# Neighbourhood attention of the second block in steps of two heads, with row-half score matmuls on split operands and one add-and-minimum instruction

## The reference

```python
s_loc = einsum(q, k_band) * scale + bias          # bias from rpb by relative row and column
s_loc = where(in_win, s_loc, -inf)                 # 16 columns around the query
s_ctx = einsum(q, k_ctx) * scale
p = softmax(concatenate([s_loc, s_ctx], -1))
o = einsum(p_loc, v_band) + einsum(p_ctx, v_ctx)
```

## Time and profile before

| | us |
|---|---|
| median of 3 runs | 3548.5 (3540.64 to 3551.41) |
| the profiled execution | 3541.35, its span 3539.6 |
| PE, PEld, DVE, ACT, POOL busy | 3237.2, 2082.1, 1327.0, 1012.4, 233.2 |

### The profile page before, as it was taken

One profiled execution on the slowest core, in us unless ns is written; L12 is line 12 of the kernel. 1 busy time (PEld: TensorE's weight loads), 2 busy tenths in 40 slices (PEclk: granted clock), 3 DMA queues, 4 the chain that ended last, 5 costly groups with the idle time before them and its releaser, 6 DMA issues.

```text
span 3539.6 us, 38820 instructions
## 1 busy us (share of the span) xinstructions
PE 3237.2 (91%) x15536; PEld 2082.1 (59%) x15536; DVE 1327.0 (37%) x2224; ACT 1012.4 (29%) x1976; POOL 233.2 (7%) x224
## 2 busy tenths in 40 slices
PE   7999979998999979988999878999999998869998
PEld 3555644534555545433666446888788565448886
DVE  2452231223552322121433754333323333563444
ACT  2452211111551211123123444222222222343332
POOL 0010000000000100000022001000001022000000
PEclk9999989998999989998999999999999999989999
DMA  4011238871002248885210001333232210013221
GB/s 165 25 37 49 72 120 356 357 323 50 35 25 78 77 200 336 366 343 211 71 36 25 13 1 72 119 119 119 109 118 76 99 41 26 1 61 105 97 95 48
DMA packets 62001, 413.62 MB, mean 117 GB/s; under 512 B 7504, under 2 KB 8016, under 8 KB 14464
## 3 DMA queue, kind: packets, MB, share of 16 engines
q1 hardware_dynamic: 55664, 392.06, 28.7%
q0 software_dynamic: 5008, 16.98, 1.4%
q10 hardware_dynamic: 1152, 2.10, 0.2%
HBM read 409.01 MB, written 2.10 MB: 116 GB/s over the span
## 4 chain that ended last, share of the span: by engine, by line
PE 85%; DVE 8%; ACT 3%; issue 2%; POOL 1%; DMA 1%; DVEq 0%; ACTq 0%; SPq 0%; POOLq 0%
PE bank L644 82%; PE bank L645 3%; DVE arena L1798 3%; ACT arena L1292 3%; DVE x L1798 1%; DMA weight<-in_ada_w 0%; POOL arena L2471 0%; POOL arena L2481 0%; POOL arena L2413 0%; DVE arena L2031 0%; DVE arena L2333 0%; DVE arena L2029 0%; DVE tokens_low L1798 0%; DMA weight<-in_w_up 0%; DVE arena L2049 0%
## 5 line engine op out<-in xcount | busy, mean ns | idle before, releaser
L644 PE MATMUL bank<-arena,weight 128*128 128x512 f32 (+2 forms) x2080 | 826.4, 555 | 59.1 <-DVE arena L1798 42.0
L1292 ACT ACTIVATE arena<-bank 128x512 f32<-128x512 f32 (+5 forms) x746 | 374.5, 520 | 1690.2 <-PE bank L644 1394.7
L644 PE MATMUL bank<-arena 128*64 128x128 f32 (+4 forms) x3888 | 620.6, 342 | 54.7 <-ACT arena L1292 23.7
L644 PEld LDWEIGHTS bank<-arena,weight 128*128 128x128 f32 (+1 forms) x2080 | 392.7, 191 | 469.9 <-issue 427.5
L644 PE MATMUL bank<-weight,arena 128*64 128x512 f32 (+5 forms) x2936 | 608.8, 530 | 33.0 <-ACT arena L1292 9.7
L644 PEld LDWEIGHTS bank<-arena 128*128 128x128 f32 (+2 forms) x3888 | 399.7, 170 | 238.5 <-issue 142.8
L644 PEld LDWEIGHTS bank<-weight,arena 128*64 128x64 f32 (+2 forms) x2936 | 294.9, 150 | 316.2 <-issue 261.3
L644 PE MATMUL bank<-hidden,weight_part 128*128 128x512 f32 (+1 forms) x2304 | 446.4, 355 | 0.0
L644 PE MATMUL bank<-tokens_high,weight_part 128*128 128x512 f32 (+1 forms) x1536 | 420.6, 359 | 23.9 <-DVE tokens_low L1798 23.7
L644 PEld LDWEIGHTS bank<-hidden,weight_part 128*128 128x128 f32 x2304 | 381.1, 189 | 70.3 <-DVE arena L1798 3.5
L644 PEld LDWEIGHTS bank<-tokens_high,weight_part 128*128 128x128 f32 x1536 | 276.5, 191 | 82.7 <-DVE tokens_low L1798 30.4
(11 more groups left out here) (115 smaller groups left out, 1676.7 us busy)
## 6 DMA issues: line engine op xcount, KB each, us to landing
weight<-in_w_gate SPq DMA_DIRECT2D x64, 1024.0 KB, 13.8
weight<-in_w_up SPq DMA_DIRECT2D x64, 1024.0 KB, 6.7
weight<-in_w_down SPq DMA_DIRECT2D x64, 1024.0 KB, 10.1
weight<-in_w_ff SPq DMA_DIRECT2D x64, 1024.0 KB, 5.0
weight<-in_ada_w SPq DMA_DIRECT2D x48, 1024.0 KB, 5.5
weight<-in_w_in SPq DMA_DIRECT2D x26, 1024.0 KB, 6.1
weight<-in_w_o SPq DMA_DIRECT2D x8, 1024.0 KB, 4.8
weight<-in_w_mem_kv SPq DMA_DIRECT2D x8, 1024.0 KB, 4.8
```

The lines of the kernel that those rows point to most:

```text
L644: mm = lambda o, a, b, first=True, last=True: eng.matmul(o, a, b, start=first, stop=last, skip_group_check=True)
L1292: act = lambda o, i, f=ACT.Copy, **k: eng.activation(o, i, f, **k)
```

## The change

In the neighbourhood attention of both layers of the second block:

- The queries are scaled by -1/8 and, like the keys, stored as a high and a low fp32r part (ACT writes the high part, DVE the low one). `Q` and the zero-padded `KZ` are gone, and POOL's clearing of `KZ` with them.
- A step is a pair of heads. The scores are three matmuls for each head on its own 64 rows, the heads taking turns, 512 columns for both heads and then 256 for both.
- The scores and the bias have the other sign: mask +1e30, `MASK - b` on POOL, and the minimum in place of the maximum. One `tensor_tensor_reduce` adds the bias and takes the minimum of 512; a second one does the 256 context scores against a zero, starting from the first one's minimum. ACT's copy, DVE's reduction over 768 and its negation are gone.
- The exponential is `exp(-x + min)` and not divided; `attend_blocks` is used, with the division at the end through `shares` and `out_scaled`. Half of the transposed tiles are copied down by DVE.
- `MASK`, the zero, the `BM` slots and `RB` lie in buffers that all stages of the block have (`AC`, `SQ`, `N`). There are still two `BM` slots, and POOL's loop is as it was but for the operation.

```diff
+                def na_score(pu):
+                    kind, _, j, q = pu
+                    at = q * P + (0 if kind == "n" else T)
+                    for name, keys in (("S", slice(0, T)), ("Sc", slice(T, T + CT))):
+                        if name == "S" and kind == "nc":
+                            continue
+                        o = [take_bank((name, u)) for u in heads_of(pu)]
+                        for n, (a, b) in enumerate((("QH", "KH"), ("QH", "KL"), ("QL", "KH"))):
+                            for h in range(2):
+                                r = slice(64 * h, 64 * h + 64)
+                                i = mm(o[h][:, 0:keys.stop - keys.start], S[a][r, j, at:at + P], S[b][r, j, keys], n == 0, n == 2)
...
+                attend_blocks(na_blocks(l), S, na_score, ..., beside(2))
...
+                def na_exps(pu):
...
+                    for u in heads_of(pu):
+                        eng.wait_ge(*after(("nb", u)))
+                        p, at = S["PR"].get(u), 2 * pu[3] + u[4]
+                        src = p if pu[0] == "n" else PB.get(("Sc", u))[:, 0:CT]
+                        act(p if pu[0] == "n" else p[:, 0:CT], src, ACT.Exp, bias=S["ST"].get(u)[:, 0:1], scale=-1.0,
+                            accum_out=r[:, at:at + 1])...
...
+                def na_tops(pu):
+                    for u in heads_of(pu):
...
+                        eng.wait_ge(*after(("out", ("S", u))))
+                        eng.wait_ge(*after(("bm", u)))
+                        eng.tensor_tensor_reduce(p[:, 0:T], PB.get(("S", u)), S["BM"].get(u), 1.0, 3.0e38, ADD, ALU.min,
+                                                 s[:, 0:1]).then_inc(*done(PB.free(("S", u)), S["BM"].free(u)))
+                        eng.wait_ge(vector_step, done.count)
+                        eng.wait_ge(*after(("out", ("Sc", u))))
+                        eng.tensor_tensor_reduce(p[:, T:T + CT], PB.get(("Sc", u))[:, 0:CT], S["ZERO"].broadcast_to([P, CT]), 1.0, s[:, 0:1], ADD, ALU.min,
+                                                 s[:, 0:1]).then_inc(*done(PB.free(("Sc", u)), ("nb", u)))
...
-                eng.memset(S["KZ"], 0.0).then_inc(*done(("nz", l)))
...
-                    eng.tensor_tensor(b, b, S["MASK"], ADD).then_inc(*done(("bm", us[n])))
+                    eng.tensor_tensor(b, S["MASK"], b, SUB).then_inc(*done(("bm", us[n])))
```

More of the change, by code:

```diff
@@ L144, in constants @@
     inside = (kc >= start) & (kc < start + 16)
-    mask = np.where(inside, 0.0, -1e30).astype(f)
+    mask = np.where(inside, 0.0, 1e30).astype(f)
     mask = np.tile(mask, (2, ROWS))
@@ L544, in build @@
             t = f".na{l}"
-            b = dict(H=H, YG=Y2, Q=c(2, T + CT), KZ=c(4, T + CT), V=c(6, 256), MASK=c(T), BM=c.ring("BM" + t, 2, T), **com)
-            b.update(attention(c, t, T + CT, 4, 5))
+            b = dict(H=H, YG=Y2, **{n: c.rounded(f"na_{n}{l}", 2, T + CT) for n in ("QH", "QL", "KH", "KL")}, V=c(6, 256),
+                     MASK=com["AC"].slots[0], ZERO=com["AC"].slots[1][:, 0:1], BM=Ring(st, "BM" + t, com["SQ"].slots), **com)
+            b.update(paired(c, t, T + CT, 4, (2, 2), [com["N"]]))
             B["na", l] = b
@@ L579, in build, with na_blocks @@
         PREP_AT = [NG - 4, NG - 2] + [NG + 4 * j + 2 * h for j in range(3) for h in range(2)]
-        def na_units(l):
-            return units("n", l, range(2), TB) + (units("nc", l, range(2), 2) if l == 0 else [])
+        def na_blocks(l):
+            return blocks_of("n", l, range(2), TB) + (blocks_of("nc", l, range(2), 2) if l == 0 else [])
         def df_units(l, j):
@@ L1184, in _ @@
                 project_rows("nv", "w_nv", 6)
-                for key in [("nqc", l, j, i) for j in range(2) for i in range(1 + both)]:
+                for key in [("nql", l, j, i) for j in range(2) for i in range(1 + both)]:
                     eng.wait_ge(*after(key))
-                for key in [("nkc", l, h, i) for h in range(4) for i in range(2)]:
+                for key in [("nkl", l, j, i) for j in range(2) for i in range(2)]:
                     eng.wait_ge(*after(key))
@@ L1356, in shares, with attend_blocks @@
                     eng.wait_ge(*after(S["RB"].former))
-                copy(b, ("rb", okey), PB.get(("rb", okey)), ("rbc", okey))
-            def attend_blocks(pus, S, n, okey, nq, between=None, turn_lag=1, value_lag=2):
+                copy(b[:, 0:nq * P], ("rb", okey), PB.get(("rb", okey))[:, 0:nq * P], ("rbc", okey))
+            def attend_blocks(pus, S, one, blocks, okey, nq, between=None, turn_lag=1, value_lag=2):
                 for i in range(len(pus) + value_lag):
@@ L1631, in _, with high @@
                 S = B["na", l]
-                eng.wait_ge(*after(("nz", l)))
-                pair_copy(S["Q"], "nq", "nqc", both)
+                def high(dst, key, scale, j, i):
+                    cols = (slice(0, T), slice(T, T + CT))[i]
+                    eng.wait_ge(*after(("out", key)))
+                    act(S[dst][:, j, cols], PB.get(key)[:, 0:(T, CT)[i]], scale=scale).then_inc(*done((key[0] + "h", l, j, i)))
                 for j in range(2):
[L1635 to L1639, removed]
+                    high("QH", ("nq", l, j), -(64 ** -0.5), j, 0)
+                    if both:
+                        high("QH", ("nq", l, j, "c"), -(64 ** -0.5), j, 1)
@@ L1640, in _ @@
+                for j in range(2):
+                    high("KH", ("nk", l, j), 1.0, j, 0)
+                    high("KH", ("nk", l, j, "c"), 1.0, j, 1)
                 for c in range(6):
                     copy(S["V"][:, c, :], ("nv", l, c), PB.get(("nv", l, c))[:, 0:256], ("nvc", l, c))
[L1643 to L1681, removed]
+                def na_exps(pu):
+                    if pu[3] == 0:
+                        S["RS"].take(okey(pu))
+                        if S["RS"].former:
+                            eng.wait_ge(*after(S["RS"].former))
+                    r = S["RS"].get(okey(pu))
+                    for u in heads_of(pu):
[3 more added lines that the diff above has]
+                        act(p if pu[0] == "n" else p[:, 0:CT], src, ACT.Exp, bias=S["ST"].get(u)[:, 0:1], scale=-1.0,
+                            accum_out=r[:, at:at + 1]).then_inc(*done(*((PB.free(("Sc", u)),) if pu[0] == "nc" else ()), S["ST"].free(u), ("e", u)))
@@ L2240, in _ @@
                 S = B["na", l]
[L2242 to L2254, removed]
-                    eng.wait_ge(vector_step, done.count)
-                    ts(s[:, 1:2], s[:, 0:1], -1.0, None, MUL).then_inc(*done(("nb", u)))
@@ new lines, in low @@
+                def low(dst, high, key, scale, j, i):
+                    cols = (slice(0, T), slice(T, T + CT))[i]
+                    eng.wait_ge(*after((key[0] + "h", l, j, i)))
+                    stt(S[dst][:, j, cols], PB.get(key)[:, 0:(T, CT)[i]], scale, S[high][:, j, cols], MUL, SUB).then_inc(*done(PB.free(key), (key[0] + "l", l, j, i)))
+                for j in range(2):
+                    low("QL", "QH", ("nq", l, j), -(64 ** -0.5), j, 0)
+                    if both:
+                        low("QL", "QH", ("nq", l, j, "c"), -(64 ** -0.5), j, 1)
```

95 lines of the change are left out of this document (49 added, 46 removed).

## The result

| | before | after |
|---|---|---|
| median of 4 runs each, same chip, us | 3547.52 (3540.64 to 3551.41) | 3567.99 (3564.44 to 3569.59) |
| the profiled execution (span), us | 3541.35 (3539.6) | 3569.5 (3567.7) |
| PE, DVE, ACT, POOL busy, us | 3237, 1327, 1012, 233 | 3243, 1285, 984, 228 |
| the stage in layer 0, layer 1, us | 89.8, 75.5 | 100.9, 86.8 |

The ratio is 1.0058, 95% interval 1.004 to 1.0076: slower by 20.5 us (14 to 27). DVE and ACT lost 42 and 28 us of work, and the kernel became slower.

The account below looks back on a forecast made before the run. PE carries 85% of the chain; after the change POOL's loop and a held bank make PE wait in the two stages. 3541.35 + 1 (order) + 18 (clock) = 3560, plus half of 7: 3564 us, range 3536 to 3584.

Parts of the forecast that it names:

- POOL's loop: Bias tiles on POOL, two slots, two DMAs and one addition: 4.1 us a head, 8.2 a pair, untouched by the change.
- The new operation: DVE's bias addition with minimum in one instruction: 0.75 us for 512 scores, 0.45 for 256.
- Rival C: DVE's new operation is slow: at 1.63 us instead of 0.75 the kernel takes 3592, at 1.1 3575; chance 0.12.
- The held bank: PE's last two transposes of a pair wait until DVE has read the second head's scores: 3.5 us gaps, steps 1 to 6.
- The order of the work without the clock: Both stages with PE's waits but no clock loss: 89.7 and 76.5 us, 0 and +1 us against before.
- The clock: PE's granted clock falls behind the gaps, 1.8 us of work lost each time: 9.2 us a layer, 18.4 in both.
- Rival A: No clock loss, PE's gaps are filled enough: 3546 us, no change; chance 0.27.
- the last step: Last step with transposes held: POOL's 8.2 us, plus 1.5 for the clock, less 1.0 because POOL is then ahead.
- Other steps: Before clock loss: step 1 11.5 and 9.8 us by layer, output tiles 13.0 and 11.3, `shares` 8.9, last pair 2.2.
- the half of 7: Profiled execution before lies 7 us below the median of its runs; half of that added to the sum of 3560.
- Rival B: PE isn't held and POOL's loop alone bounds: 3523 us, 3527 with the half, not below 3523; chance 0.11.

Follow-up runs that it names:

- e1_fill: The changed kernel with the second head's first four transposes issued six times where PE waits ahead of its last two; 3547.52 us, ratio 1.0009.
- e3_bm4: The changed kernel with four slots for the bias tile instead of two; 3502.72 us, ratio 0.9883.
- e2_values_first: The changed kernel with PE's values and `shares` of a step issued ahead of its transposes; 3555.04 us, ratio 1.0031.

## Why the prediction was right, step by step

Forecast 3564 with 3536 to 3584; measured 3568.0. Direction and mechanism held, and the size came out with some help of luck; some terms of the sum were off.

- **POOL's loop**, 4.1 us for a head: 4.04 to 4.13 in pairs 0 to 5, 4.29 and 4.26 in pair 6, 1.85 and 1.70 in the last (2.2 forecast). The rows of the kernel before had the loop whole, since POOL's instructions changed only in their operation, at 1.28 us as before. The new operation takes 0.69 us, not 0.75; the read of its accumulator lies within its last 0.08 us. Rival C, a slow operation, is out. And POOL's two DMAs still take 1.36 us with the long multiplication on DVE gone. That lock between the two engines, which the Trainium skill describes ("SBUF — State Buffer", "SBUF: two separate sides"), gave nothing back here, as the row without DVE work had said.
- **The held bank**, gaps of 3.5 us in steps 1 to 6: six in each layer, 2.9 to 3.6 us. e1_fill shows the clock's part of the cost, e3_bm4 what goes when the waits go too.
- **The order of the work without the clock**: 0 and +1 us. e1_fill puts it at +2.3 and +3.1 by the stages, or at +0.7 and +1.5 without the 1.6 us that each of its ends is longer. Its steps of layer 0 take 8.1, 11.4, 13.2, 13.2, 8.3, 8.8 and 9.1 against 8.2, 11.5, 13.0, 13.0, 8.2, 8.9 and 8.2.
- **The clock**: 18.4 us forecast. Filling the gaps brought 20.5 by medians, 17 by the ratios and 17.1 by the stages, or 20.2 with the 3.1 that e1_fill lost at its own ends. Step 3 of layer 0 shows the size of one: values 2.83 instead of 1.53 and tiles 0.3 above, and the next pair's first head comes 14.81 us behind this one's where I had 13.0 + 1.8. Filled, it is 13.2. Single steps lost 1.1 to 2.8 us where I had 1.5 and 1.8 (without the last one): step 1 of layer 0 2.6, the steps with `shares` 2.8 and 2.6. Rival A, no clock loss, is out by e1_fill alone. The Trainium skill ("TensorE: Matmul & The Clock Gate", "HAM oscillation — how this bites in real kernels") has a loop that loses its clock again in every turn; its waits are for DMAs, the ones here for a bank. The trace agrees: in the 5 us behind each of the twelve gaps the clock is 0.50 to 0.72.
- **Mis-sized: the last step.** I had 8.2 for POOL's pair, 1.5 for the clock, and gave 1.0 back "because POOL is then ahead". It isn't ahead. The two DMAs of the last tile come apart (0.69, 0.56 of issue, 0.69: 1895.37 to 1897.31), and the step is 9.0 to 9.1 us in e1_fill, where the clock stays at 1.00. The kernel before has that already (POOL's DMAs from 2943.55 to 2945.52). With PE's scores at half clock from 1897.20 on, the step took 9.39 and 9.57 where my terms give 8.7. So the clock's share of it, 0.3 and 0.5, was about right, by a wrong reason; POOL's 8.2 was 0.9 short.
- **Other steps.** Step 1 of layer 0 was 0.7 longer than forecast, step 2 of layer 1 0.9, the step with `shares` 0.9 and 0.6, most of it clock as above; step 1 of layer 1 was 0.5 shorter, the last pair and the end 0.6 in layer 0 and 1.2 in layer 1. The stages came to 100.9 and 86.8 against 98.9 and 85.7.
- **The median.** The profiled execution was 1.5 us above the median of its runs this time, where that of before was 6 below. But the sum for the profiled execution, 3560, was 9 us low: 3 in the stages, the rest outside of them, in the scatter named above. The median came within 4 us because of the half of 7 and because the profiled execution lay above its median this time, and that is luck.
- **Rival B**, faster because PE isn't held, did not happen by this change, and its floor was wrong as a statement on the design. It had POOL's loop as a bound of 3523. With one more slot the loop itself opens, and the kernel runs at 3508, with two at 3503. I had named the two slots as what the change leaves alone, and had not asked what they were worth.

Not tried: separate banks for scores and transposes, which by the order of the takes should free T1b with two slots; output tiles moved into the gap; five or more slots. Why some steps lost 2.5 to 2.8 us by the clock and others 1.1 to 1.9 stays open.

## What to carry to other kernels

Where a producer's load for the next tile waits for the slot just read, add up the loop of read, issue, load and work before you make the consumer cheaper: at 4.02 us beside a unit of 4.24 it was hidden by 0.2, and a change that took 42 us off DVE cost 20 with two slots and brought 38 with four. Where a step takes all the banks of a ring, look for the take that comes round to a bank of the same step, and at all that is queued behind it. And price a wait of PE by the clock behind it as well: behind twelve waits of about 3.3 us the lower clock cost 17 to 20 us, on top of the 45 that went when the waits themselves went.

## What the runs showed of the hardware

- 240 transposes of no use made a kernel 17 (ratios) to 20.5 us (medians) faster, by holding the granted clock at 0.96 to 0.98 instead of 0.80 to 0.85. In the 5 us behind each of the twelve gaps of 2.9 to 3.6 us it was 0.50 to 0.72. Behind eleven gaps of 1.15 to 1.38 us in e1_fill it stayed at 1.00; behind one of 0.9 with one of 1.4 to 1.5 us after it, it was 0.66, in both layers. Gaps of 1.9 to 2.1 us did both, 1.00 or 0.66, in the kernel before and in e2_values_first.
- A bias addition with a minimum over 512 columns, in one DVE instruction, takes 692 ns where the addition alone takes 0.68 to 0.69 us; over 256 columns 484 ns.
- fp32 matmuls on the two row halves run side by side, too: 8 records for a pair, four of 512 and four of 256 columns, in 1.56 us, where one after another they would take 2.56 (an estimate, at 0.427 for a record of 512 and half for 256).
